# The start of a decoder kernel: first two row tiles multiplied before their norm is known

## Chip, core and metric

The kernel runs on one core of a Trainium2 chip. The metric is the device time of one execution in microseconds; the time before is 1604.12 us, the median of three runs.

## What is computed

One decoder layer on 1024 prompt rows and 8 sample rows of width 1024, all in 32-bit floats. Only the beginning of the mixer matters here: the rows are normed (rms norm with gain `mix_pre_g`), multiplied by `w_in`, and the second 1024 columns of the product, v, go through gelu and layer norm.

```python
def rms_norm(x, g):
    xf = x.astype(jnp.float32)
    y = xf * lax.rsqrt(jnp.mean(xf * xf, axis=-1, keepdims=True) + EPS)
    return (y * g.astype(jnp.float32)).astype(x.dtype)
...
    z = jnp.einsum("btd,dc->btc", xn, w_in)
    u, v, b_gate, c_gate, x_in, r_a, r_b = jnp.split(z, SPLITS, axis=-1)
    u = jax.nn.gelu(u)
    v = layer_norm(jax.nn.gelu(v), sgu_ln_g, sgu_ln_b)
    y_a = jnp.einsum("btc,cd->btd", u * chunk_spatial_mix(v, w_s, b_s), w_a_out)
```

The rest of the layer (the other parts of z, a short convolution, three output products, a gated feed-forward net) follows and is not changed.

## The kernel before

Every product of 32-bit numbers is made of three products of a faster format: each operand is split into a high part (a copy in the format f32r, made by ScalarE) and a low part (the number less its high part, made by VectorE or GpSimd), and high times high, low times high and high times low are added up in PSUM.

The program writes each engine's order out by hand; engines meet at counting semaphores. The stage at issue works through nine row tiles, `V_TILES`: position i = 0 is the tile of 8 sample rows, i = 1 to 8 are the prompt tiles of 128 rows. For each of them:

- SyncE's queue loads the rows (`x_load(i)`), into one of two buffers `x_rows`, and `wv_load(k)` loads the eight pieces of v's weight, 512 KB each, into `gv`.
- ScalarE sums the squares (`square(i)`) and splits off the high part of each weight piece (`wv_split(k)`).
- VectorE works out the reciprocal root in seven or eight one-column instructions (`row_root`), scales the rows by root and gain (`scale_rows(i)`, into `x_norm`), and makes the low parts of the weight (`wv_rest(k)`).
- TensorE turns the scaled rows, eight blocks (`turn_norm(i)`), ScalarE copies the high part from PSUM (`norm_split(i)`), VectorE makes the low part (`xn_rest(i)`, into `tp`).
- TensorE multiplies: `v_sample_tile` for the samples in the order of the table `V_STEPS`, `v_first_tile(1)` and `(2)` with all high products of a tile ahead of its low ones, then `v_tile(3)` to `(8)`, which wait for the low part before they start (`pe.wait_ge(xn_lo_done, i + 1)`). Each makes 48 products of 512 columns, and the turns of the next tile stand among them.
- ScalarE applies gelu and writes v, VectorE norms it (`v_layer_norm(i)`).

For VectorE the order from the second prompt tile on is this loop; the samples' own norm, with its gain and bias, is its pass i = 0:

```python
for i in range(9):
    if 0 < i < 8:
        xn_rest(i + 1)
    if 0 < i < 7:
        scale_rows(i + 2)
    if i < 8:
        v_layer_norm(i)
```

GpSimd has little to do here: it makes the identity matrix, copies the samples' split parts into `tp`, and masks `ws_rows`. Before its first real work TensorE turns the identity 32 times and 11 times (`turn_ident`).

Of the kernel before, what the change touches and what calls it, by code (L numbers as in the profile page):

```python
# [126 lines left out]
V_STEPS = [(0, 0), (0, 1), (1, 0), (0, 2), (1, 1), (0, 3), (1, 2), (0, 4), (1, 3), (0, 5), (0, 6), (1, 4), (0, 7), (1, 5), (1, 6), (1, 7)]  # L127
# [11 lines left out]
def build(nc, x_prompt, x_sample, state_conv, mix_pre_g, mix_post_g, w_in, sgu_ln_g, sgu_ln_b, w_s,  # L139
# [16 lines left out]
    with ctx:  # L156
# [62 lines left out]
        ws00 = at("ws00", sa_at + 1024, [128, KT])  # L219
        tail_out = s_bc[0:(2 + NS) * KT, 1].rearrange("p a c -> p (a c)")[:, 0:128]  # L220
# [12 lines left out]
        eps, warm = small[:, 46:47], small[:, 47:48]  # L233
        ps = ctx.enter_context(nc.psum_tensor("ps", [128, 8, 512], f32))
# [115 lines left out]
        wv_hi, wv_lo = sem("wv_hi"), sem("wv_lo")  # L350
# [58 lines left out]
        def _(pe):  # L409
# [7 lines left out]
            def turn_norm(i):  # L417
                rows = rows_of(V_TILES[i])
                pe.wait_ge(x_scaled, i + 1)
                if i >= 2:  # L420
                    pe.wait_ge(xn_lo_done, i - 1)
                for k in range(KT):
                    at_k = k ^ 1 if i and not home(V_TILES[i])[0] else k
                    ins = pe.transpose(ps[:, xn_bank(i) + k // 4, 128 * (at_k % 4):128 * (at_k % 4) + rows],  # L424
                                       x_norm[i % 2][0:rows, 128 * k:128 * k + 128], ident[0:rows, 0:rows])
                ins.then_inc(norm_turned, 1)

            def v_tile(i):
                t = V_TILES[i]
                pe.wait_ge(xn_lo_done, i + 1)  # L430
                if i >= 2:
                    pe.wait_ge(v_gelu, i - 1)
                for k in range(KT):
                    if k == 4 and i + 1 < 9:
                        turn_norm(i + 1)
                    outs = [ps[0:rows_of(t), 2 * (i % 2) + n, :] for n in range(2)]
                    w_h, w_l = ([w[:, k, 512 * n:512 * n + 512] for n in range(2)] for w in (wv_hi_t, wv_lo_t))
                    ins = three(outs, *xn_parts(t, k), w_h, w_l, k == 0, k == KT - 1)
                ins.then_inc(v_full, 1)

# [11 lines left out]
            def v_sample_tile():  # L452
                pe.wait_ge(xn_lo_done, 1)
                for low, k in V_STEPS:
                    x_h, x_l = xn_parts(8, k)
                    if low:
                        if k == KT - 2:
                            turn_norm(1)
                        pe.wait_ge(wv_lo, k + 1)
                        ins = wv_products(0, x_h, wv_lo_t, k, False, k == KT - 1)  # L460
                    else:
                        pe.wait_ge(wv_hi, k + 1)
                        wv_products(0, x_h, wv_hi_t, k, k == 0, False)
                        wv_products(0, x_l, wv_hi_t, k, False, False)
                ins.then_inc(v_full, 1)

            def v_first_tile(i):
                t = V_TILES[i]
                pe.wait_ge(xn_hi_done, i + 1)
                if i >= 2:  # L470
                    pe.wait_ge(v_gelu, i - 1)
# [302 lines left out]
        def _(sp):  # L774
            def x_load(i):
                t = V_TILES[i]
                if i >= 2:
                    sp.wait_ge(x_scaled, i - 1)
# [37 lines left out]
            x_load(0)  # L816
            sp.dma_start(pre_gain[0:NS, :], mix_pre_g[0:1, :].to_broadcast((NS, D))).then_inc(pre_first, 16)
            for k in range(KT):
                if k == 4:
                    x_load(1)  # L820
# [10 lines left out]
            sp.dma_start(ws_rows[:, :].rearrange("p (h j) -> p h j", h=KT), w_s[0].rearrange("h i j -> i h j")).then_inc(ws_in, 16)  # L831
            sp.dma_start(mix_b[:, :, :].rearrange("p h i -> p (h i)"),
# [6 lines left out]
            sp.dma_start(conv_sample[0, :, 0, :], state_conv[0, :, 1, :]).then_inc(hist_saved, 16)  # L839
            load(0)  # L840
# [227 lines left out]
        def _(pool):  # L1068
# [5 lines left out]
                               pattern=[[-1, 128]], channel_multiplier=1).then_inc(consts, 1)  # L1074
            for part, (smp, ready) in enumerate(((smp_hi, xn_hi_done), (smp_lo, xn_lo_done))):
# [124 lines left out]
        def _(act):  # L1200
# [15 lines left out]
            def norm_split(i):  # L1216
                act.wait_ge(norm_turned, i + 1)
# [45 lines left out]
            square(2)  # L1263
            for i in range(9):
                if 0 < i < 8:
                    norm_split(i + 1)
                if 0 < i < 7:
                    square(i + 2)
                act.wait_ge(v_full, i + 1)
                if i == 1:  # L1270
                    act.wait_ge(wv_lo, KT)
                rows = rows_of(V_TILES[i])
                dst = gv[:, V_TILES[i], :] if i else v_smp[0:NS, :]
                act.activation(dst.rearrange("p (a n) -> p a n", a=2), ps[0:rows, 2 * (i % 2):2 * (i % 2) + 2, :],
                               ACT.Gelu_apprx_tanh).then_inc(v_gelu, 1)
# [431 lines left out]
        def _(dve):  # L1707
# [16 lines left out]

            def row_root(i):
                rows = rows_of(V_TILES[i])
                a, y, w = (small[0:rows, 20 + n:21 + n] for n in range(3))
# [4 lines left out]
            def scale_rows(i, rooted=False):  # L1732
                rows, y = rows_of(V_TILES[i]), small[0:rows_of(V_TILES[i]), 21:22]
# [31 lines left out]

            scale_rows(0)
            wv_rest(0)
            xn_rest(0)
            for k in range(1, 4):
                wv_rest(k)  # L1770
            row_root(1)
            for k in range(4, 7):
                wv_rest(k)
            scale_rows(1, rooted=True)
            wv_rest(7)
            xn_rest(1)
            scale_rows(2)
            for i in range(9):
                if 0 < i < 8:
                    xn_rest(i + 1)  # L1780
                if 0 < i < 7:
                    scale_rows(i + 2)
                if i < 8:
                    v_layer_norm(i)
                if i == 0:
                    dve.wait_ge(v_norm, 1)
                    dve.wait_ge(ln_in, 32)
                    link(dve.tensor_tensor(v_smp[0:NS, :], v_smp[0:NS, :], ln_g[0:NS, :], MUL))
                    dve.tensor_tensor(v_smp[0:NS, :], v_smp[0:NS, :], ln_b[0:NS, :], ADD).then_inc(vs_ready, 1)
# [811 lines left out]
```

## Time and profile before

| what | value |
|---|---|
| time, median of 3 runs | 1604.12 us (1603.16 to 1604.5) |
| span of the profiled execution | 1601.0 us |
| TensorE busy | 1590.6 us, 99% |
| VectorE, ScalarE, GpSimd busy | 68%, 35%, 44% |

The profile gives the span of the profiled execution, from its first to its last instruction, and no separate time for it; the runs' median is 3.1 us above that span. In the rows further down PE is TensorE, DVE VectorE, ACT ScalarE, POOL GpSimd and SP SyncE. All starts are in us from the start of the span.

### The profile page before, as it was taken

How to read it: one execution, taken by the hardware profiler on the slowest of the kernel's cores; microseconds unless marked ns; L12 is line 12 of the kernel's file. 1: busy time of each engine (PE TensorE's matmuls, PEld its weight loads, DVE VectorE, ACT ScalarE, POOL GpSimd, SP SyncE). 2: the span in 40 equal slices, each digit the busy share in tenths (PEclk: the TensorE clock that was granted, in tenths of full speed). 3: DMA queues.
4: the chain of work that ended last, by engine and by line, in shares of the span. 5: the costliest groups of instructions: out<-in, count | busy, mean ns of one | idle time of the engine just before them, and what ended most of it. 6: DMA issues, size and time to landing. Idle time of an engine off the chain costs nothing.

```text
span 1601.0 us, 30253 instructions
## 1 busy us (share of the span) xinstructions
PE 1590.6 (99%) x12427; PEld 1542.2 (96%) x12427; DVE 1081.9 (68%) x1463; ACT 559.8 (35%) x852; POOL 703.9 (44%) x512
## 2 busy tenths in 40 slices
PE   9999999999999999999999999999999999999998
PEld 6889999999999999999978999999999999999997
DVE  8757857797793338868965666766666666575766
ACT  4222332222223336333434532333332233352544
POOL 1011534544544444644730324544444443545375
PEclk9999999999999999999999999999999999999999
DMA  6202011431423333474423313533333345472723
GB/s 216 79 1 80 27 54 34 126 96 44 126 82 110 109 106 121 149 242 133 148 91 120 131 41 110 155 105 100 106 104 104 105 124 178 153 239 80 238 107 133
DMA packets 155283, 184.38 MB, mean 115 GB/s; under 512 B 7355, under 2 KB 138035, under 8 KB 155147
## 3 DMA queue, kind: packets, MB, share of 16 engines
q1 hardware_dynamic: 154987, 182.41, 35.7%
q8 instruction: 99, 1.62, 0.4%
q14 instruction: 37, 0.30, 0.1%
q10 hardware_dynamic: 160, 0.04, 0.0%
HBM read 133.74 MB, written 48.72 MB: 114 GB/s over the span
## 4 chain that ended last, share of the span: by engine, by line
PE 95%; DVE 1%; DMA 1%; POOL 1%; issue 1%; SPq 0%; ACT 0%; DVEq 0%; ACTq 0%; POOLq 0%
PE ps L414 91%; PE ps L449 1%; PE ps L526 1%; DMA pre_gain<-in_mix_pre_g 1%; DVE tp L2213 1%; PE ps L669 0%; PE ps L653 0%; PE ps L424 0%; DMA tp_f<-hid_dram 0%; SPq L783 0%; DVE s_bc L2232 0%; POOL ring_lo L1108 0%; POOL ring_lo L1095 0%; PE ps L503 0%; DVE g L2234 0%
## 5 line engine op out<-in xcount | busy, mean ns | idle before, releaser
L414 PE MATMUL ps<-tp,ring_hi 128*128 128x258 f32 x7292 | 1182.9, 283 | 0.5 <-issue 0.3
L414 PEld LDWEIGHTS ps<-tp,ring_hi 128*128 128x128 f32 x7292 | 1010.6, 190 | 0.9 <-issue 0.5
L414 PE MATMUL ps<-tp,ring_lo 128*128 128x258 f32 x3646 | 744.8, 283 | 0.0
L414 PEld LDWEIGHTS ps<-tp,ring_lo 128*128 128x128 f32 x3646 | 571.3, 190 | 0.0
L1095 POOL TENSOR_TENSOR ring_lo<-ring_f,ring_hi 128x512 fp32r<-128x512 f32 (+1 forms) x228 | 328.3, 1460 | 365.1 <-DVE ring_f L1840 212.5
L1095 POOL TENSOR_TENSOR ring_lo<-stage,ring_hi 128x512 fp32r<-128x512 f32 (+1 forms) x199 | 304.7, 1540 | 400.3 <-ACT ring_hi L1240 399.6
L1240 ACT ACTIVATE ring_hi<-ring_f 128x512 fp32r<-128x512 f32 (+1 forms) x228 | 142.6, 627 | 519.9 <-DVE ring_f L1835 196.2
L1240 ACT ACTIVATE ring_hi<-stage 128x512 fp32r<-128x512 f32 (+1 forms) x199 | 122.0, 617 | 121.1 <-PE ps L414 63.5
L1832 DVE TENSOR_TENSOR ring_f<-stage 128x512 f32<-128x512 f32 (+1 forms) x57 | 46.8, 821 | 135.2 <-PE ps L414 82.7
L1853 DVE TENSOR_TENSOR s_a<-ps,s_a 128x516 f32<-128x516 f32 (+1 forms) x58 | 39.8, 686 | 51.9 <-PE ps L414 51.4
L414 PE MATMUL ps<-tp 128*128 128x512 f32 (+1 forms) x384 | 72.0, 340 | 0.0
L414 PEld LDWEIGHTS ps<-tp 128*128 128x128 f32 x384 | 59.0, 189 | 8.2
L2385 DVE TENSOR_TENSOR tp<-tp_f,tp 128x2064 fp32r<-128x2064 f32 (+1 forms) x24 | 56.2, 2343 | 13.7 <-ACT tp L1583 13.7
L1251 ACT ACTIVATE s_a<-ps 128x516 f32<-128x516 f32 (+1 forms) x58 | 34.2, 590 | 77.3 <-PE ps L414 60.2
L1864 DVE TENSOR_TENSOR s_a<-ps,s_a 128x516 f32<-128x516 f32 (+1 forms) x58 | 39.6, 683 | 30.5 <-PE ps L414 30.4
L1583 ACT ACTIVATE tp<-tp_f 128x2064 fp32r<-128x2064 f32 (+1 forms) x24 | 42.8, 1784 | 39.8 <-DMA tp_f<-hid_dram 33.2
L414 PE MATMUL ps<-wv_hi_t,tp 128*128 128x512 f32 x192 | 54.1, 397 | 0.0
L2420 DVE TENSOR_TENSOR hq<-hq,q 128x516 f32<-128x516 f32 x40 | 47.0, 1176 | 1.1
L1835 DVE TENSOR_TENSOR ring_f<-ring_f,stage 128x512 f32<-128x512 f32 (+1 forms) x57 | 42.8, 751 | 2.2 <-PE ps L414 2.2
L414 PEld LDWEIGHTS ps<-wv_hi_t,tp 128*128 128x128 f32 x192 | 35.7, 188 | 8.0
L1837 DVE TENSOR_TENSOR ring_f<-stage 128x512 f32<-128x512 f32 (+1 forms) x57 | 39.6, 695 | 0.0
L1847 DVE TENSOR_TENSOR s_bc<-ps,s_a 128x516 f32<-128x516 f32 (+1 forms) x21 | 14.0, 668 | 36.8 <-PE ps L414 36.6
(243 smaller groups left out, 1453.9 us busy)
## 6 DMA issues: line engine op xcount, KB each, us to landing
stage<-in_w_in SPq DMA_DIRECT2D x24, 1024.0 KB, 5.9
ht_dram<-ht SPq DMA_DIRECT2D x44, 258.0 KB, 4.2
hid_dram<-hq SPq DMA_DIRECT2D x40, 258.0 KB, 3.1
stage<-in_w_gate SPq DMA_DIRECT2D x10, 1024.0 KB, 6.6
stage<-in_w_up SPq DMA_DIRECT2D x10, 1024.0 KB, 5.3
tp_f<-hid_dram SPq DMA_DIRECT2D x16, 516.0 KB, 5.5
tp_f<-ht_dram SPq DMA_DIRECT2D x16, 516.0 KB, 8.7
stage<-in_w_down SPq DMA_DIRECT2D x8, 1024.0 KB, 7.1
```

The costliest lines, as they stand in the source:

```text
L414: ins = pe.matmul(o, w, xc, start=first and n == 0, stop=last and n == 2)
L1095: pool.tensor_tensor(lo, src, hi.bitcast(f32), SUB).then_inc(w_lo, 1)
L1240: act.activation(w_ring(b, p, kp)[0], src, ACT.Copy).then_inc(w_hi, 1)
L1251: act.activation(s_a[:, gs], reg(Z, gs), ACT.Copy).then_inc(s1_done, 1)
L1583: act.activation(slot(s, 0, both, ks), slot_f(s, 1, both, ks), ACT.Copy).then_inc(t_hi, 1)
L1832: ins = dve.tensor_tensor(out, a21, a22, ADD)
L1835: ins = dve.tensor_tensor(out, ring(ring_f, b, 1, kp), a11, SUB)
L1837: ins = dve.tensor_tensor(out, a11, a21, SUB)
L1853: dve.tensor_tensor(s_a[:, gs], reg(X, gs), s_a[:, gs], ADD).then_inc(u1_done, 1)
L1864: dve.tensor_tensor(s_a[:, gs], reg(Z, gs), s_a[:, gs], ADD).then_inc(u2_done, 1)
L2385: dve.tensor_tensor(slot(s, 1, both, ks), slot_f(s, 1, both, ks), slot_v(s, 0, both, ks), SUB).then_inc(t_lo, 1)
L2420: dve.tensor_tensor(hq[:, n], hq[:, n], q[:, n], MUL).then_inc(hid_ready, 1)
```

## The change

The samples and the first prompt tile are no longer scaled by their root before the product. The raw rows are turned at once (`turn_raw`), multiplied by the gain (turned into one column for each block, `gain_cols`), split, and multiplied; the root is applied as the scale of the gelu that reads the product. The normed, turned rows are still made as before, since later stages use them. Further:

- The samples' high parts (columns 0 to 7) and low parts (columns 32 to 39) stand in one tile, `smp_v`, of 40 columns, so that one product with the high weight gives both; the two groups of result rows are added afterwards, by a copy on ScalarE and a sum on VectorE.
- The steps of samples and first prompt tile are one table, `V_STEPS`: S is the 40-column product with a high weight piece, s the samples' with a low piece, H, L and l the prompt tile's three products, N a `turn_norm`; each of S, s, H, L, l is two products of 512 columns.
- GpSimd makes the low parts of weight pieces 3, 5 and 7; VectorE keeps 0, 1, 2, 4 and 6.
- The turns of the identity fall from 43 to 16.
- In VectorE's order the samples' layer norm stands behind `scale_rows(3)`.
- In SyncE's queue the first prompt tile is loaded right after the first weight piece; `x_load` of later tiles, `mix_b` and `load(0)` wait for the new steps.

```diff
-V_STEPS = [(0, 0), (0, 1), (1, 0), (0, 2), (1, 1), (0, 3), (1, 2), (0, 4), (1, 3), (0, 5), (0, 6), (1, 4), (0, 7), (1, 5), (1, 6), (1, 7)]
+V_STEPS = "S0 s0 S1 H0 H1 s1 S2 H2 L0 S3 H3 L1 S4 H4 s2 S5 H5 L2 s3 N0 H6 s4 S7 H7 s5 s6 L3 L4 L5 s7 S6 " \
+          "l0 l1 l2 N1 l3 l4 l5 L6 N2 L7 l6 l7".split()
+RAW_TURNS, RAW_SCALES = 2, 3
+WV_POOL = (3, 5, 7)
+WV_DVE = (0, 1, 2, 4, 6)
...
+            def v_start():
+                pe.wait_ge(consts, 5)
+                pe.wait_ge(x_scaled, 2)
+                for n, step in enumerate(V_STEPS):
+                    what, k = step[0], int(step[1])
+                    if what == "N":
+                        turn_norm(k)
+                    elif what == "S":
+                        pe.wait_ge(wv_hi, k + 1)
+                        ins = raw_products(32 + NS, 0, smp_v[:, k, :], wv_hi_t, k, n == 0, k == 6)
+                        if k == 6:
+                            ins.then_inc(v_full, 1)
+                    elif what == "s":
+                        wv_low_ready(k)
+                        raw_products(NS, 0, smp_v[:, k, 0:NS], wv_lo_t, k, False, False)
+                    elif what == "H":
+                        pe.wait_ge(raw_high, 1)
+                        pe.wait_ge(wv_hi, k + 1)
+                        raw_products(128, 2, raw_hi[:, k, :], wv_hi_t, k, k == 0, False)
+                    elif what == "L":
+                        pe.wait_ge(v_norm, 1)
+                        raw_products(128, 2, raw_lo[:, k, :], wv_hi_t, k, False, False)
                     else:
...
+                        wv_low_ready(k)
+                        ins = raw_products(128, 2, raw_hi[:, k, :], wv_lo_t, k, False, k == 7)
...
+            def turn_raw():
+                pe.wait_ge(x_in[0], 16)
+                pe.wait_ge(gain_in, 16)
+                for k in range(KT):
+                    pe.transpose(ps[:, 6, NS * k:NS * k + NS], x_rows[0][0:NS, 128 * k:128 * k + 128], ident[0:NS, 0:NS])
+                pe.transpose(ps[:, 6, NS * KT:NS * KT + KT], gain_rows[:, :], ident[0:KT, 0:KT]).then_inc(norm_turned, 1)
+                turn_ident(8)
+                pe.wait_ge(x_in[1], 16)
+                for k in range(KT):
+                    ins = pe.transpose(ps[:, 4 + k // 4, 128 * (k % 4):128 * (k % 4) + 128], x_rows[1][:, 128 * k:128 * k + 128], ident[:, :])
+                ins.then_inc(norm_turned, 1)
...
-            turn_ident(32)
-            turn_norm(0)
-            turn_ident(11)
-            v_sample_tile()
-            v_first_tile(1)
+            turn_ident(8)
+            turn_raw()
+            v_start()
             v_first_tile(2)
...
+            pool.memset(smp_v[:, :, NS:32].bitcast(f32), 0.0).then_inc(consts, 1)
+            for k in WV_POOL:
+                pool.wait_ge(wv_hi, k + 1)
+                pool.tensor_tensor(wv_lo_t[:, k, :], gv[:, k, :], wv_hi_t[:, k, :].bitcast(f32), SUB).then_inc(wv_lo_pool, 1)
...
             square(0)
             wv_split(0)
+            square(1)
             wv_split(1)
-            wv_split(2)
+            act.wait_ge(x_scaled, 3)
+            act.activation(raw_hi[:, :, :], raw_x[:, :, :], ACT.Copy).then_inc(raw_high, 1)
+            for k in range(2, KT):
+                wv_split(k)
             norm_split(0)
-            wv_split(3)
-            square(1)
-            for k in range(4, KT):
-                wv_split(k)
+            square(2)
+            act.wait_ge(v_full, 1)
+            act.activation(v_smp[0:NS, :].rearrange("p (a n) -> p a n", a=2), ps[32:32 + NS, 0:2, :], ACT.Copy).then_inc(v_gelu, 1)
             norm_split(1)
...
+            def v_norm_sample():
+                v_layer_norm(0)
+                dve.wait_ge(v_norm, 3)
+                dve.wait_ge(ln_in, 32)
+                link(dve.tensor_tensor(v_smp[0:NS, :], v_smp[0:NS, :], ln_g[0:NS, :], MUL))
+                dve.tensor_tensor(v_smp[0:NS, :], v_smp[0:NS, :], ln_b[0:NS, :], ADD).then_inc(vs_ready, 1)
...
+            wv_rest(0)
+            dve.wait_ge(norm_turned, 2)
+            dve.tensor_tensor(raw_x[:, :, :], bank_pair(4), gain_cols.unsqueeze(2).to_broadcast((128, KT, 128)), MUL).then_inc(x_scaled, 1)
+            wv_rest(1)
+            raw_rest()
+            wv_rest(2)
             scale_rows(0)
-            wv_rest(0)
+            wv_rest(4)
+            wv_rest(6)
+            row_root(1)
             xn_rest(0)
...
             scale_rows(1, rooted=True)
-            wv_rest(7)
+            scale_rows(2)
+            dve.wait_ge(v_gelu, 1)
+            dve.tensor_tensor(v_smp[0:NS, :].rearrange("p (a n) -> p a n", a=2), ps[0:NS, 0:2, :],
+                              v_smp[0:NS, :].rearrange("p (a n) -> p a n", a=2), ADD).then_inc(v_norm, 1)
             xn_rest(1)
-            scale_rows(2)
-            for i in range(9):
-                if 0 < i < 8:
+            for i in range(1, 9):
+                if i < 8:
                     xn_rest(i + 1)
-                if 0 < i < 7:
+                if i < 7:
                     scale_rows(i + 2)
+                if i == 1:
+                    v_norm_sample()
                 if i < 8:
                     v_layer_norm(i)
```

TensorE, the middle of the start sequence. Before, samples (`smp_hi`, `smp_lo`) are multiplied alone, and prompt products (`tp`) follow:

```order
L449 MATMUL ps<-wv_hi_t,smp_hi 8x512 x2
L449 MATMUL ps<-wv_hi_t,smp_lo 8x512 x2
L449 MATMUL ps<-wv_lo_t,smp_hi 8x512 x2
L424 MATMUL ps<-ident,x_norm_83 128x128 x8
L449 MATMUL ps<-wv_lo_t,smp_hi 8x512 x4
L449 MATMUL ps<-wv_hi_t,tp 128x512 x18
L449 MATMUL ps<-wv_lo_t,tp 128x512 x2
```

Now the steps from s3 to S6, with the turn of the samples' normed rows (`x_norm_82`) among them:

```order
L472 MATMUL ps<-wv_lo_t,smp_v 8x512 x2
L438 MATMUL ps<-ident,x_norm_82 128x8 x8
L472 MATMUL ps<-wv_hi_t,raw_hi 128x512 x2
L472 MATMUL ps<-wv_lo_t,smp_v 8x512 x2
L472 MATMUL ps<-wv_hi_t,smp_v 40x512 x2
L472 MATMUL ps<-wv_hi_t,raw_hi 128x512 x2
L472 MATMUL ps<-wv_lo_t,smp_v 8x512 x4
L472 MATMUL ps<-wv_hi_t,raw_lo 128x512 x6
L472 MATMUL ps<-wv_lo_t,smp_v 8x512 x2
L472 MATMUL ps<-wv_hi_t,smp_v 40x512 x2
```

Products of the prompt tile moved between those of the samples, and each product waits for its own weight part.

VectorE, around the samples' layer norm. Before, its last three passes (`v_smp`) stand directly ahead of the low part of the second prompt tile (`tp`):

```order
L1764 TENSOR_SCALAR v_smp<-v_smp,small 8x1024
L1788 TENSOR_TENSOR v_smp<-v_smp,ln_g 8x1024
L1789 TENSOR_TENSOR v_smp<-v_smp,ln_b 8x1024
L1752 TENSOR_TENSOR tp<-ps,tp 128x2x4x128
```

Now, with the one-column instructions of the roots left out at the dots, two low parts stand ahead of the scaling of the third prompt tile (`x_norm_83`), the samples' norm and that of the first tile (`gv`) behind it, and the next low part last:

```order
L1866 TENSOR_TENSOR v_smp<-ps,v_smp 8x1024
L1820 TENSOR_TENSOR tp<-ps,tp 128x2x4x128 x2
...
L1808 SCALAR_TENSOR_TENSOR x_norm_83<-x_rows_81,small,pre_gain 128x1024
L1826 BN_STATS small<-v_smp 8x6
...
L1832 TENSOR_SCALAR v_smp<-v_smp,small 8x1024
L1842 TENSOR_TENSOR v_smp<-v_smp,ln_g 8x1024
L1843 TENSOR_TENSOR v_smp<-v_smp,ln_b 8x1024
L1826 BN_STATS small<-gv 128x6
...
L1832 TENSOR_SCALAR gv<-gv,small 128x1024
L1820 TENSOR_TENSOR tp<-ps,tp 128x2x4x128
```

The samples' norm moved from ahead of the low part of the second prompt tile to ahead of that of the third.

## Rows read from the trace of the kernel before

**Rows 1.** The page: busy time (first three engines), and the chain by engine.

```profile
PE 1590.6 (99%) x12427; PEld 1542.2 (96%) x12427; DVE 1081.9 (68%) x1463; ACT 559.8 (35%) x852; POOL 703.9 (44%) x512
PE 95%; DVE 1%; DMA 1%; POOL 1%; issue 1%; SPq 0%; ACT 0%; DVEq 0%; ACTq 0%; POOLq 0%
```

**Rows 2.** TensorE's timeline (start, us, what), then a piece of the chain in time order.

```profile
1.76 5.87 PE L509 MATMUL ps<-ident 128*128 128x128 f32 x32 [1.76 <-POOL ident L1073]
...
9.35 0.69 PE L449 MATMUL ps<-wv_hi_t,smp_hi 128*8 128x512 f32 x2
...
22.05 4.46 PE L449 MATMUL ps<-wv_hi_t,tp 128*128 128x512 f32 x18 [0.19 <-ACT tp L1221]
...
34.16 4.34 PE L449 MATMUL ps<-wv_hi_t,tp 128*128 128x512 f32 x18
...
46.15 0.62 PE L414 MATMUL ps<-wv_hi_t,tp 128*128 128x512 f32 x2
...
52.71 11.17 PE ps L414 x48
```

**Rows 3.** Timeline of VectorE.

```profile
9.21 3.48 DVE L1744 TENSOR_TENSOR wv_lo_t<-gv,wv_hi_t 128x1024 fp32r<-128x1024 f32 x3
...
26.41 0.67 DVE L1758 BATCH_NORM_STATS2 small<-v_smp 8x6 f32<-8x512 f32 x1
...
30.73 1.21 DVE L1788 TENSOR_TENSOR v_smp<-v_smp,ln_g 8x1024 f32<-8x1024 f32 x1
31.98 2.09 DVE L1789 TENSOR_TENSOR v_smp<-v_smp,ln_b 8x1024 f32<-8x1024 f32 x1
34.00 1.21 DVE L1752 TENSOR_TENSOR tp<-ps,tp 128x1024 fp32r<-128x1024 f32 x1
...
38.37 0.69 DVE L1758 BATCH_NORM_STATS2 small<-gv 128x6 f32<-128x512 f32 x1
...
42.75 1.23 DVE L1752 TENSOR_TENSOR tp<-ps,tp 128x1024 fp32r<-128x1024 f32 x1
```

**Rows 4.** Timeline of ScalarE at the first weight pieces.

```profile
5.31 1.06 ACT L1214 ACTIVATE wv_hi_t<-gv 128x1024 fp32r<-128x1024 f32 x1 [1.39 <-DMA gv<-in_w_in]
6.58 1.06 ACT L1214 ACTIVATE wv_hi_t<-gv 128x1024 fp32r<-128x1024 f32 x1 [0.22 <-DMA gv<-in_w_in]
```

**Rows 5.** GpSimd's passes and VectorE's beside them, from five places.

```profile
9.10 3.65 POOL L1080 CAST tp<-smp_hi 128x16 fp32r<-128x16 f32 x4 [7.39 <-ACT smp_hi L1219]
31.91 1.09 POOL L1083 TENSOR_SCALAR_AFFINE_SELECT ws_rows<-ws_rows 128x1024 f32<-128x1024 f32 x1 [18.61 <-DMA ws_rows<-in_w_s]
110.43 3.00 POOL L1095 TENSOR_TENSOR ring_lo<-stage,ring_hi 128x512 fp32r<-128x512 f32 x2 [77.43 <-ACT ring_hi L1240]
110.64 0.27 DVE L1722 TENSOR_SCALAR small<-small 128x1 f32<-128x1 f32 x1
133.52 2.31 DVE L1806 TENSOR_TENSOR tp_f<-tp_f,tp 128x2064 f32<-128x2064 f32 x1
134.53 3.72 POOL L1095 TENSOR_TENSOR ring_lo<-stage,ring_hi 128x512 fp32r<-128x512 f32 x2 [18.61 <-ACT ring_hi L1240]
137.12 1.15 DVE L1891 TENSOR_TENSOR mix_s<-mix_s,q 128x4 f32<-128x4 f32 x1
138.87 0.15 DVE L1891 TENSOR_TENSOR mix_s<-mix_s,q 128x4 f32<-128x4 f32 x1
147.87 2.54 POOL L1095 TENSOR_TENSOR ring_lo<-stage,ring_hi 128x512 fp32r<-128x512 f32 x2 [9.61 <-ACT ring_hi L1240]
164.90 4.52 DVE L1821 TENSOR_TENSOR tp<-tp_f,tp 128x2064 fp32r<-128x2064 f32 x2
166.25 4.30 POOL L1095 TENSOR_TENSOR ring_lo<-stage,ring_hi 128x512 fp32r<-128x512 f32 x1 [7.76 <-ACT ring_hi L1240]
```

**Rows 6.** Stretches: us, TensorE busy (products and turns), other engines, PEclk, DMA, GB/s.

```profile
2.00:4.00 2.00, 2.00 (x11) 2.00 (x11) 0.06 (x1) 1.44 (x4) 0.00 (x0) 1.00 0.77 162
7.00:8.00 1.00, 1.00 (x13) 0.83 (x12) 1.00 (x2) 0.77 (x2) 0.00 (x0) 1.00 1.01 414
```

More of the change, by code:

```diff
@@ L450, in wv_products, with wv_low_ready @@
                 return ins
[L452 to L460, printed above, removed]
-                    else:
[L462 to L465, printed above, removed]
+            def wv_low_ready(k):
+                if k in WV_POOL:
+                    pe.wait_ge(wv_lo_pool, WV_POOL.index(k) + 1)
+                else:
+                    pe.wait_ge(wv_lo, WV_DVE.index(k) + 1)
@@ new lines, in raw_products @@
+            def raw_products(rows, bank, x, w, k, first, last):
+                for n in range(2):
+                    ins = pe.matmul(ps[0:rows, bank + n, :], x, w[:, k, 512 * n:512 * n + 512], start=first, stop=last)
+                return ins
+            def v_start():
[20 more added lines that the diff above has]
+                        raw_products(128, 2, raw_lo[:, k, :], wv_hi_t, k, False, False)
+                    else:
+                        wv_low_ready(k)
+                        ins = raw_products(128, 2, raw_hi[:, k, :], wv_lo_t, k, False, k == 7)
+                        if k == 7:
+                            ins.then_inc(v_full, 1)
@@ L816, in _ @@
             x_load(0)
+            sp.dma_start(gain_rows[:, :], mix_pre_g[0].rearrange("(k p) -> k p", p=128)).then_inc(gain_in, 16)
+            wv_load(0)
+            x_load(1)
+            wv_load(1)
             sp.dma_start(pre_gain[0:NS, :], mix_pre_g[0:1, :].to_broadcast((NS, D))).then_inc(pre_first, 16)
-            for k in range(KT):
-                if k == 4:
-                    x_load(1)
+            for k in range(2, KT):
                 wv_load(k)
@@ L839, in _ @@
             sp.dma_start(conv_sample[0, :, 0, :], state_conv[0, :, 1, :]).then_inc(hist_saved, 16)
+            sp.wait_ge(v_full, 2)
             load(0)
@@ L1268, in _ @@
                     square(i + 2)
+                rows = rows_of(V_TILES[i])
+                if i == 0:
+                    act.wait_ge(v_norm, 2)
+                    act.wait_ge(x_scaled, 1 + RAW_SCALES)
+                    act.activation(v_smp[0:NS, :], v_smp[0:NS, :], ACT.Gelu_apprx_tanh, scale=small[0:NS, 10:11]).then_inc(v_gelu, 1)
+                    continue
                 act.wait_ge(v_full, i + 1)
+                dst = gv[:, V_TILES[i], :].rearrange("p (a n) -> p a n", a=2)
+                src = ps[0:rows, 2 * (i % 2):2 * (i % 2) + 2, :]
                 if i == 1:
[L1271 to L1275, printed above, removed]
+                    act.wait_ge(wv_lo, len(WV_DVE))
+                    act.wait_ge(wv_lo_pool, len(WV_POOL))
+                    act.wait_ge(x_scaled, 2 + RAW_SCALES)
+                    act.activation(dst, src, ACT.Gelu_apprx_tanh, scale=small[:, 11:12]).then_inc(v_gelu, 1)
+                else:
+                    act.activation(dst, src, ACT.Gelu_apprx_tanh).then_inc(v_gelu, 1)
                 if i == 7:
@@ L1723, in newton, with root_of @@
                 link(dve.tensor_scalar(y, t, 1.5, y, ADD, MUL))
+            def root_of(i):
+                col = 10 + i if i < 2 else 21
+                return small[0:rows_of(V_TILES[i]), col:col + 1]
             def row_root(i):
                 rows = rows_of(V_TILES[i])
-                a, y, w = (small[0:rows, 20 + n:21 + n] for n in range(3))
+                a, y, w = small[0:rows, 20:21], root_of(i), small[0:rows, 22:23]
                 dve.wait_ge(sumsq, i + 1)
@@ L1732, in scale_rows @@
             def scale_rows(i, rooted=False):
-                rows, y = rows_of(V_TILES[i]), small[0:rows_of(V_TILES[i]), 21:22]
+                rows, y = rows_of(V_TILES[i]), root_of(i)
                 if not rooted:
```

60 lines of the change are left out of this document (34 added, 26 removed).

## The prediction

> **What bounds the kernel now.** The page's first lines and the chain that ended last come first: TensorE is busy 99% of the span and holds 95% of the chain [rows 1]. Whatever keeps TensorE's first products waiting is therefore paid in full at the end, and whatever the other engines save is worth nothing unless TensorE starts or continues earlier. Everything that the change touches lies ahead of 110 us. The timeline of TensorE there [rows 2] shows warm-up turns from 1.76 us, the sample products from 9.35, the first prompt tile's from 22.05, the second's from 34.16, the third's from 46.15 (12.0 us for a tile: later tiles show 11.17 for their 48 products, 0.465 for a pair, and the rest, 0.8 to 0.9, are the eight turns). There is one idle piece, 0.19 us. I call the point at 46.15 T: the products of `v_tile(3)` begin there, from there on nothing in the kernel changes, and TensorE has no idle time behind it in which a shift could be lost. So the forecast is the new T less 46.15.
>
> The timeline of VectorE [rows 3] tells what T hangs on. `v_tile(3)` waits for the fourth low part of turned rows (`xn_rest(3)`), which VectorE starts at 42.75 and ends near 43.95: 2.2 us of slack. VectorE was continuously busy from 34.00 to that point: low part, root and scale 4.37 (until 38.37), layer norm 4.38 (until 42.75). Its passes of 1024 columns take 1.16 each (3.48 for three).
>
> **What the change removes from TensorE.** A sample step was two high, two low-operand and two low-weight products; now the 40-column operand makes one pair do the first two. Sixteen of 96 products go, 8 pairs, 3.7 us. Samples and first tile are then 40 pairs, 18.5 us, plus three turns, some 2.4: 20.9 us. The start is nearer too: the second x piece is now requested before the second weight piece; in the old order the first two pieces of 512 KB landed at 5.31 and 6.58 [rows 4], so it should land near 6.6 and weight piece 1 at 7.9. Eight raw turns end at 7.5, VectorE's scaling of the raw tile at 8.7, and ScalarE, whose split of weight piece 1 ends at 8.95, makes the high part by 10.0. The first sample and prompt pairs run between; from 10.0 on 37 pairs and 2.4 us of turns are left, 19.5 us. If nothing else were late, the first tile would end at 29.6 instead of 34.16, a gain of 4.6 us.
>
> **What VectorE has to do.** It loses three weight low parts (3 x 1.16) to GpSimd and gets the scaled raw tile, its low part and the sum of the sample halves (1.16 each) and four small instructions (my estimate, 0.9 in all, from the 0.15 and 0.27 of the small passes in [rows 5]). It comes out even. But the order moves: the layer norm of the samples, 7.6 us in the old timeline (26.41 to 34.00, of which 0.9 is explained below), stood before `xn_rest(2)` and ended at 34.00, while TensorE was in the first prompt tile. Now it stands between `scale_rows(3)` and the first tile's layer norm, both ahead of `xn_rest(3)`. From the high part of tile 1 on, VectorE does 4.37 (low part, root, scale) + 6.8 (samples' norm: 4.32 to 30.73, then twice 1.24) + 4.38 + 1.18 = 16.7 us, and TensorE has only the second prompt tile, 12.0, before it needs the result. Since the high part comes 1.06 us after turn N2, and N2 is followed by three pairs (1.4 us), the end of the start sequence, E, gives T = E - 0.3 + 16.7 = E + 16.4, against E + 12.0 before. Of the 4.6 us gained, 4.4 are given back: T = 46.0, no change. This holds without any contention.
>
> **GpSimd's three low parts.** How GpSimd and VectorE meet is in [rows 5]. Alone, two passes of 512 columns took 2.54 us, 1.27 each. At 134.53 the same two took 3.72: the first began while VectorE's pass of two SBUF inputs (133.52 to 135.83) was running and got through only after it. At 137.12 VectorE's four-column pass, 0.15 us when repeated at 138.87, took 1.15 under GpSimd's second. At 31.98 the 8-row addition took 2.09 against 1.21 for the multiplication before it [rows 3], beside GpSimd's 1.09 pass at 31.91. The one-column passes of the roots are not held: at 110.64 one took its 0.27 under GpSimd's pass of 110.43. So passes with two SBUF inputs exclude each other. The Trainium skill says so too, in SBUF — State Buffer, section SBUF: two separate sides: the port pair shared by VectorE and GpSimd is an exclusive lock held for a whole instruction. By that rule the sum is the one below, without it the 46.0 above; the trace agrees with the rule.
>
> A low part of 1024 columns on GpSimd is not in the trace: twice 1.27 is 2.5, which I take; with overhead shared 2.3; from the pair at 110.43 (3.00, with VectorE beside it) 3.0. Who goes first when both wait? Casts of GpSimd got in between back-to-back VectorE passes of the same form as here (four in 3.65 us from 9.10, while VectorE ran three), but once a pass was held until the second of two VectorE passes ended (4.30 at 166.25, those from 164.90 to 169.42). I take turn and turn about. The walk: weight low part 2 on VectorE ends at 12.5; GpSimd's part 3 has it until 15.0; `scale_rows(0)`, ready at 14.4, until 16.2; part 5 until 18.7; VectorE's part 4 until 19.8; part 7 until 22.3; part 6 until 23.5. VectorE has waited 0.6 + 2.5 + 2.5 = 5.6 us. Then root and scale of rows 1 and 2 (with the samples' low part, 0.22) until 30.2, sum of samples 31.4, `xn_rest(1)` 32.5. TensorE waits 1.3 for part 4 (at 19.9) and 1.8 for part 6 (until 23.5), turns N2 at 30.4 and ends E near 32.2. ScalarE is held as well: its gelu of the samples waits for the sum (31.4 to 32.4), so the high part of tile 1 is ready at 33.4. T = 33.4 + 16.7 = 50.1, and TensorE has waited 0.7 and 4.7 more. That is +4.0.
>
> **The clock.** The granted clock reads 1.00 throughout, but the turns of `turn_ident` show two levels: 11 in 2 us at 2 to 4 us, 13 in 1 us at 7 to 8 [rows 6], by their ratio the levels 1.2 and 2.4 GHz; up to that rise TensorE had worked without a gap since 1.76. The new start has 16 such turns, not 43, and gaps. If the level is still low at 6.6, the raw turns cost 1.6 instead of 0.9 and everything behind them moves 0.6. I take half, 0.3. The Trainium skill (TensorE: Matmul & The Clock Gate, Part 1) has the throttled state as the default that activity releases, which would make these gaps count; the sum here goes by the rows.
>
> **Sum.** +4.0 + 0.3 = +4.3 us. The span was 1601.0, the median of the runs 1604.12, 3.1 above it; the same stands around both. Predicted 1608.4.
>
> **Rivals.**
> 1. VectorE keeps the port while it has work, as at 166.25: it does `scale_rows(0)` and parts 4 and 6 in a row until 18.5, GpSimd's part 5 ends at 21.0 and part 7 near 24.7. VectorE waits 0.6 + 0.3 + 0.5 only, TensorE 1.1 and 1.4; E is 32.1, T 48.5: +2.3, with the clock 2.6. 1606.7. For it the one row, against it the casts.
> 2. The port costs nothing here, T 46.0 (or GpSimd's parts come in VectorE's root chains): 1604 to 1605. Three places in [rows 5] speak against it.
> 3. The clock falls again in the wait of 4.7 us before T, or in those of 1.3 and 1.8. The trace has no such wait to price it; the first low stretch, from 1.76 to some point between 4 and 7, cost half of its length, 1.1 to 2.6 us, and I take as much for each fall: 1610 to 1613.
> 4. Faster: the 4.6 us are kept, 1599.5. That needs VectorE to reach `xn_rest(3)` before TensorE has done the second tile, so a tail of at most 12.3 us behind the high part of tile 1; the rows make it 16.7. It would come out so only if VectorE ran the sample norm inside its earlier idle time, which its program order excludes. Even with no wait at all VectorE's own passes from 7.5 add to some 36 us, T 43.9, 2.2 us of gain.
>
> **How the numbers follow.** Forecast (turn and turn about, 1607.8 for GpSimd passes of 2.3 to 1609.9 for 3.0, the clock's 0.3 included) 0.50; rival 1 0.20; rival 2 0.13; rival 3 0.12; rival 4 0.05. A measurement tells this kernel from no change at about 0.2%, 3.2 us. Slower by more: the forecast but for its low end (0.47), rival 3 (0.12), the upper end of rival 1 (0.04): 0.63. Faster by more 0.05. Same 0.32. The range leaves out rival 4 and part of rivals 2 and 3: 1604.8 to 1611.0.
>
> **What would show it.** The start sequence without the port would end at 29.6; I expect 32 to 33. VectorE's parts 4 and 6 (or GpSimd's 5 and 7) stretched to 3 us or more, TensorE idle 1 to 2 us before two low-weight pairs of the samples. Before `v_tile(3)` one wait of 4 to 5 us for VectorE's `tp`, T near 50. If that wait is absent, the step on the moved norm is wrong; if the parts are not stretched, that on the port. Turns of 0.2 us at 6.6 show the low clock.

## The result, and the profile after

The changed kernel takes 1610.12 us (median of five runs, 1609.24 to 1610.3) against 1604.12 before: ratio 1.0036, 95% interval 1.0024 to 1.0048. It is 6.0 us slower. Forecast were 4.3 us, with a range that ends at 1611.0.

The page after, the same two lines as in [rows 1]:

```profile
PE 1590.2 (99%) x12401; PEld 1541.8 (96%) x12401; DVE 1083.6 (67%) x1467; ACT 561.5 (35%) x854; POOL 711.1 (44%) x516
PE 93%; DVE 3%; POOL 1%; DMA 1%; issue 1%; ACT 1%; SPq 0%; DVEq 0%; ACTq 0%; POOLq 0%
```

TensorE's busy time hardly falls, though 16 products and 27 turns of the identity are gone (17 turns of raw rows and gain have come): some of its instructions ran slower. VectorE's share of the chain, 1% before, is 3%: the path leaves TensorE and goes through VectorE for some 17 us.

TensorE's timeline after, to be held against [rows 2]:

```profile
6.74 1.97 PE L512 MATMUL ps<-ident,x_rows 128*128 128x128 f32 x8
8.36 1.10 PE L472 MATMUL ps<-wv_hi_t,smp_v 128*40 128x512 f32 x2
...
11.12 1.19 PE L472 MATMUL ps<-wv_hi_t,raw_hi 128*128 128x512 f32 x4 [0.73 <-ACT raw_hi L1311]
...
24.77 0.64 PE L472 MATMUL ps<-wv_lo_t,smp_v 128*8 128x512 f32 x2 [0.90 <-POOL wv_lo_t L1127]
...
32.04 4.36 PE L461 MATMUL ps<-wv_hi_t,tp 128*128 128x512 f32 x18
...
48.61 1.22 PE L426 MATMUL ps<-wv_hi_t,tp 128*128 128x512 f32 x2 [4.41 <-DVE tp L1820]
49.63 1.05 PE L426 MATMUL ps<-wv_lo_t,tp 128*128 128x512 f32 x2
50.48 1.91 PE L426 MATMUL ps<-wv_hi_t,tp 128*128 128x512 f32 x4
```

The second prompt tile starts at 32.04, 2.1 us earlier than before; the third at 48.61, 2.5 us later, behind one wait of 4.41 us for VectorE. And the products behind the wait are slow: pairs start 0.85 to 1.02 us apart, not 0.46. In the chain (start, us, what) the 24 products ahead of the next turns took 8.11 us (7.95 in the timeline, from 48.61 to the turns at 56.56):

```profile
47.42 1.15 DVE tp L1820
48.57 0.04 issue
48.61 8.11 PE ps L426 x24
56.72 0.87 PE ps L438 x8
```

Before, the 24 products between 46.15 and the next turns took 5.5. So the second half of the third tile starts at 57.60 against 52.71 [rows 2]: 4.9 us are lost there, 2.46 because the tile starts later and 2.4 by slow products.

VectorE's timeline after, against [rows 3]:

```profile
15.32 1.50 DVE L1808 SCALAR_TENSOR_TENSOR x_norm<-x_rows,small,pre_gain 8x1024 f32<-8x1024 f32 x1
16.75 2.34 DVE L1812 TENSOR_TENSOR wv_lo_t<-gv,wv_hi_t 128x1024 fp32r<-128x1024 f32 x2
...
31.91 1.23 DVE L1820 TENSOR_TENSOR tp<-ps,tp 128x1024 fp32r<-128x1024 f32 x1 [1.48 <-ACT tp L1274]
...
36.30 0.67 DVE L1826 BATCH_NORM_STATS2 small<-v_smp 8x6 f32<-8x512 f32 x1
...
41.87 1.21 DVE L1843 TENSOR_TENSOR v_smp<-v_smp,ln_b 8x1024 f32<-8x1024 f32 x1
43.01 0.68 DVE L1826 BATCH_NORM_STATS2 small<-gv 128x6 f32<-128x512 f32 x1
...
47.34 1.22 DVE L1820 TENSOR_TENSOR tp<-ps,tp 128x1024 fp32r<-128x1024 f32 x1
```

From the low part of the second prompt tile at 31.91 to TensorE's start at 48.61 are 16.7 us without a gap in VectorE.

GpSimd's three low parts, each from its own stretch of the timeline:

```profile
13.05 2.69 POOL L1127 TENSOR_TENSOR wv_lo_t<-gv,wv_hi_t 128x1024 fp32r<-128x1024 f32 x1 [11.14 <-ACT wv_hi_t L1267]
15.71 5.64 POOL L1127 TENSOR_TENSOR wv_lo_t<-gv,wv_hi_t 128x1024 fp32r<-128x1024 f32 x1
21.32 3.39 POOL L1127 TENSOR_TENSOR wv_lo_t<-gv,wv_hi_t 128x1024 fp32r<-128x1024 f32 x1
```

The second was next at 15.71, when the first had ended, and itself ended at 21.35. VectorE's three passes of 15.32 to 19.09 (the scaling and two low parts, without a gap) went first; it ended 2.3 us after them. VectorE itself was hardly held: its two parts took 2.34 us, 1.17 each against 1.16 in [rows 3].

Last the stretches of TensorE's slow products (columns as in [rows 6]), after:

```profile
44.00:48.60 4.60, 0.20 (x1) 0.00 (x0) 4.25 (x13) 1.02 (x1) 0.00 (x0) 0.80 0.20 71
48.60:52.00 3.40, 3.39 (x8) 2.71 (x9) 3.12 (x10) 0.00 (x0) 0.00 (x0) 0.50 0.00 0
52.00:56.00 4.00, 4.00 (x15) 3.16 (x15) 3.65 (x12) 0.00 (x0) 0.00 (x0) 0.80 0.41 135
```

The granted clock stands at 0.50, 1.2 GHz, from 48.6 to 52. It fell in the wait: the mean of the stretch that holds the wait is already 0.80.

### The profile page after: what moved, and what is told of

The parts are those of the page before. It is cut to its first block, busy times and chain, and to the rows that moved or that the text cites. A ratio compares the mean times of both kernels' runs of the same rounds, so it can differ in the third digit from the quotient of the medians.

```text
span 1608.4 us, 30225 instructions
## 1 busy us (share of the span) xinstructions
PE 1590.2 (99%) x12401; PEld 1541.8 (96%) x12401; DVE 1083.6 (67%) x1467; ACT 561.5 (35%) x854; POOL 711.1 (44%) x516
## 4 chain that ended last, share of the span: by engine, by line
PE 93%; DVE 3%; POOL 1%; DMA 1%; issue 1%; ACT 1%; SPq 0%; DVEq 0%; ACTq 0%; POOLq 0%
PE ps L426 90%; PE ps L571 1%; POOL wv_lo_t L1127 1%; DVE tp L2301 1%; DMA stage<-in_w_in 1%; PE ps L714 0%; PE ps L698 0%; PE ps L438 0%; DMA tp_f<-hid_dram 0%; DMA x_rows<-in_x_prompt 0%; POOL ring_lo L1148 0%; PE ps L472 0%; DVE s_bc L2320 0%; POOL ring_lo L1161 0%; DVE small L1786 0%
```

## The experiments

Single runs lie up to 1 or 2 us to either side of their median, so medians and intervals of 5 to 11 runs are compared, each with runs of the kernel before on the same chip. Differences to the changed kernel are differences of medians from two chips; where one is under 1 us, the traces are the better witness.

**The samples' norm moved again (e1).** It is cut in two and goes behind the first tile's:

```diff
-                if i == 1:
-                    v_norm_sample()
+                if i == 2:
+                    v_layer_norm(0)
+                if i == 3:
+                    v_gain_sample()
                 if i < 8:
                     v_layer_norm(i)
```

> The changed kernel with the samples' layer norm moved once more and cut in two: its norm stands in VectorE's pass 2, its gain and bias in pass 3. Theory A (VectorE's own chain from the high part of prompt tile 1 on, 16.7 us, is what TensorE waits for): the wait of 4.4 us before the third prompt tile's products is gone, they begin at E + 12.0 = 44.0 us, the clock does not fall, and both costs (4.4 and 2.5 us) come back: about 1603 us, some 7 us less than the changed kernel and 1 us less than the one before. Rival B (the start is late because GpSimd and VectorE hold each other's port, and the norm's place only hides that): the wait stays at 2 us or more, 1606 us or more. If the slack that remains in passes 2 and 3 is too small, a wait of about 1 us moves to the fourth or fifth tile.

Measured: 1602.44 us against 1603.91, ratio 0.999 (0.9981 to 0.9999), 7.7 us less than the changed kernel. TensorE's timeline at the third tile:

```profile
43.83 0.63 PE L461 MATMUL ps<-wv_lo_t,tp 128*128 128x512 f32 x2
44.30 0.62 PE L426 MATMUL ps<-wv_hi_t,tp 128*128 128x512 f32 x2
44.77 0.63 PE L426 MATMUL ps<-wv_lo_t,tp 128*128 128x512 f32 x2
```

No wait, no slow products, and none at the fourth or fifth tile either. The whole loss was the place of this norm; the start itself, with its wait of 0.88 us for GpSimd's last part, is 1.85 us earlier at the third tile than before (44.30 against 46.15).

**All weight low parts on VectorE (e2),** in the changed kernel:

```diff
-WV_POOL = (3, 5, 7)
-WV_DVE = (0, 1, 2, 4, 6)
+WV_POOL = ()
+WV_DVE = (0, 1, 2, 3, 4, 5, 6, 7)
...
             wv_rest(2)
+            wv_rest(3)
             scale_rows(0)
-            wv_rest(4)
-            wv_rest(6)
+            for k in range(4, KT):
+                wv_rest(k)
             row_root(1)
```

> The changed kernel with all eight weight low parts on VectorE, in the order of the pieces; GpSimd makes none. Theory A: the wait of 0.9 us for GpSimd's last part goes, VectorE has 3.5 us more to do and ends its second scaling near 29, still ahead of turn N2, so the tail is the same: 1609 to 1610.5 us, within 1 us of the changed kernel. Rival B (the port held the start back): the start sequence ends 2 us earlier or more and the time falls by as much, 1608 us or less.

Measured: 1609.41 us, ratio to before 1.0035 (1.0022 to 1.0047). TensorE:

```profile
48.74 0.79 PE L426 MATMUL ps<-wv_hi_t,tp 128*128 128x512 f32 x2 [4.40 <-DVE tp L1820]
49.33 1.05 PE L426 MATMUL ps<-wv_lo_t,tp 128*128 128x512 f32 x2
```

The same wait, at the same place. Taking GpSimd's three parts away does not make T earlier. The clock fell here too, but only behind the wait: the first pair is still fast, the second slow, and the two stretches read 1.00 and then 0.60 (columns as in [rows 6]):

```profile
44.00:48.60 4.60, 0.34 (x2) 0.00 (x0) 4.25 (x12) 1.02 (x1) 0.00 (x0) 1.00 0.15 49
48.60:52.00 3.40, 3.26 (x9) 2.58 (x10) 3.12 (x11) 0.00 (x0) 0.00 (x0) 0.60 0.02 5
```

**TensorE kept busy in the wait (e3).**

```diff
+            turn_ident(36)
             for i in range(3, 9):
                 v_tile(i)
```

> The changed kernel with 36 turns of the identity ahead of the third prompt tile's products, inside the wait of 4.4 us: TensorE's work and the point at which those products can begin (48.6 us) are the same, but it is not idle. Theory C (2.5 of the 6 us are the clock that fell in the wait): the 24 products behind the wait take 5.6 us instead of 8.1 and the time falls by 2.5, to 1607.6 us. Rival (the slow products have another cause, such as reading data just written): they stay at 8.1 us and the time at 1610 us.

Measured: 1605.95 us, ratio 1.0013 (1.0004 to 1.0022), 4.2 less than the changed kernel by the medians. TensorE's timeline:

```profile
44.11 4.09 PE L556 MATMUL ps<-ident 128*128 128x128 f32 x36
48.67 0.73 PE L426 MATMUL ps<-wv_hi_t,tp 128*128 128x512 f32 x2 [0.47 <-DVE tp L1821]
49.24 0.62 PE L426 MATMUL ps<-wv_lo_t,tp 128*128 128x512 f32 x2
```

The stretch in which the clock was 0.50 (columns as in [rows 6]):

```profile
48.60:52.00 3.40, 3.33 (x14) 2.74 (x15) 3.12 (x11) 0.00 (x0) 0.00 (x0) 1.00 0.00 0
```

The products begin at 48.67, no earlier than the 48.61 of the changed kernel, at a granted clock of 1.00; the 24 take 5.8 us in the chain. The next tile half starts at 55.32 in its chain instead of 57.60: 2.3 us, the size expected. The medians say more than the trace; the chip of this comparison gave some 0.2 us of it (its runs of before are 0.2 faster), the rest stays open.

**Only the norm moved, in the kernel before (e4).** Its first loop pass has no `v_layer_norm(0)`; norm, gain and bias stand in pass 1 behind `scale_rows(3)`:

```diff
-                if i < 8:
-                    v_layer_norm(i)
-                if i == 0:
+                if i == 1:
+                    v_layer_norm(0)
                     dve.wait_ge(v_norm, 1)
...
+                if 0 < i < 8:
+                    v_layer_norm(i)
```

> The kernel before with only the samples' norm, gain and bias moved behind the scaling of the third prompt tile. Theory A: VectorE's chain from the high part of prompt tile 1 (30.7 us) is 16.7 us long, so the third tile's products begin at 47.5 instead of 46.15 us, a wait of 1.3 us; the clock holds: 1605.4 us. Rival B: no wait, 1604.1 us.

Measured: 1605.91 us, ratio 1.0014 (1.0005 to 1.0023), 2.0 us more than before. TensorE:

```profile
47.33 0.73 PE L414 MATMUL ps<-wv_hi_t,tp 128*128 128x512 f32 x2 [1.17 <-DVE tp L1752]
```

Expected were 1.3 us of wait at 47.5. Where TensorE comes later to this place, the same tail costs only what sticks out; the granted clock stays at 1.00 through this wait of 1.17 us. The third tile starts 1.2 us later than before; the rest of the 2.0 is not traced to a place, and the interval (0.8 to 3.7 us) includes 1.2.

**All low parts on VectorE, with the norm cut in two (e5).** The norm as in e1, and the edit of e2:

```diff
-WV_POOL = (3, 5, 7)
-WV_DVE = (0, 1, 2, 4, 6)
+WV_POOL = ()
+WV_DVE = (0, 1, 2, 3, 4, 5, 6, 7)
```

> The kernel with the samples' norm cut in two, and all eight weight low parts on VectorE. TensorE is now the bound of the tail, so its own waits count: the wait of 0.9 us for GpSimd's last part goes, a wait of 0.15 at turn N2 and one of 0.7 ahead of the second prompt tile (seen in the trace with the late norm) come. Theory A: the same as with GpSimd's parts, within 0.5 us, some 1602.2 us; handing three parts to GpSimd buys nothing. Rival: VectorE, loaded with 3.5 us more, makes TensorE wait 2 us or more: 1604 us.

Measured: 1602.32 us against 1603.65, ratio 0.9992 (0.9983 to 1.0001); e1 had 0.999. TensorE has the two waits that were expected, and none for a part:

```profile
29.09 1.09 PE L438 MATMUL ps<-ident,x_norm 128*128 128x128 f32 x8 [0.23 <-DVE x_norm L1808]
32.29 4.42 PE L461 MATMUL ps<-wv_hi_t,tp 128*128 128x512 f32 x18 [0.71 <-ACT tp L1274]
```

Handing three parts to GpSimd buys nothing: its late part costs 0.9 us, VectorE's load without it 0.9, and the third tile starts at 44.36 against 44.30 in e1.

**s7 later (e6),** on top of e1:

```diff
-V_STEPS = "S0 s0 S1 H0 H1 s1 S2 H2 L0 S3 H3 L1 S4 H4 s2 S5 H5 L2 s3 N0 H6 s4 S7 H7 s5 s6 L3 L4 L5 s7 S6 " \
-          "l0 l1 l2 N1 l3 l4 l5 L6 N2 L7 l6 l7".split()
+V_STEPS = "S0 s0 S1 H0 H1 s1 S2 H2 L0 S3 H3 L1 S4 H4 s2 S5 H5 L2 s3 N0 H6 s4 S7 H7 s5 s6 L3 L4 L5 l0 l1 s7 S6 " \
+          "l2 N1 l3 l4 l5 L6 N2 L7 l6 l7".split()
```

> The kernel with the samples' norm cut in two, and in the table of steps l0 and l1 ahead of s7 and S6. Theory A: the 0.9 us in which TensorE waited for GpSimd's last part are filled by the two pairs, and the time falls by 0.9, to 1601.5 us. Rival: the samples' result comes no later, but ScalarE and VectorE behind it (copy, sum, gelu, high part of tile 1) are now the bound and the second prompt tile waits for them: 1602.4 us, no gain.

Measured: 1601.51 us against 1603.65, ratio 0.9984 (0.9976 to 0.9993). TensorE at the place of the old wait:

```profile
23.66 1.07 PE L472 MATMUL ps<-wv_lo_t,raw_hi 128*128 128x512 f32 x4
24.73 0.62 PE L472 MATMUL ps<-wv_lo_t,smp_v 128*8 128x512 f32 x2
25.19 0.62 PE L472 MATMUL ps<-wv_hi_t,smp_v 128*40 128x512 f32 x2
```

The 0.9 us are gone, and the third tile starts at 43.04, 1.3 us ahead of e1. The medians agree, but the intervals of e1 and e6 overlap. Of the kernels run this has the lowest ratio to the one before, 2.1 us by the medians, with e7 within its noise. At the third tile it is 3.1 us ahead of the kernel before, so about 1 us does not reach the end: its trace has later waits of 0.8 and 0.5 us where before has 0.3 and 0.3.

**More full turns first (e7),** on top of e1: 16 turns ahead of the samples' and 2 behind, instead of 8 and 8.

```diff
-                turn_ident(8)
+                turn_ident(2)
                 pe.wait_ge(x_in[1], 16)
...
             pe.wait_ge(consts, 4)
-            turn_ident(8)
+            turn_ident(16)
             turn_raw()
```

> The kernel with the samples' norm cut in two, and the 16 turns of the identity all but two ahead of the samples' turns, so that TensorE turns full blocks without a gap until 5.2 us. Theory C (the low clock at the start is the price of less work in its first microseconds; before the change the turns were fast from 6.3 us on, after it only from 9.3): the raw turns at 6.7 us take 0.9 instead of 1.6 us, the first pair 0.5 instead of 0.9, and the raw tile's chain starts 0.4 to 0.8 us earlier, the time falls by up to that, to 1602 us; the wait for GpSimd's last part may take it back. Rival: the clock rises at 9.3 us again: 1602.4 us.

Measured: 1601.5 us, ratio 0.9986 (0.9977 to 0.9995). But the trace does not show what the theory says. TensorE:

```profile
6.90 1.91 PE L512 MATMUL ps<-ident,x_rows 128*128 128x128 f32 x8
8.47 1.20 PE L472 MATMUL ps<-wv_hi_t,smp_v 128*40 128x512 f32 x2
9.47 0.82 PE L472 MATMUL ps<-wv_lo_t,smp_v 128*8 128x512 f32 x2
```

The raw turns take 1.9 us as before this edit, the first pair is slow, and the third tile starts within 0.2 us of e1's (44.17). The time is below both forecasts, but the interval overlaps that of e1. The theory on where the early clock comes from is not supported.

**GpSimd's three parts alone, in the kernel before (e8).**

```diff
+            for k in WV_POOL:
+                pool.wait_ge(wv_hi, k + 1)
+                pool.tensor_tensor(wv_lo_t[:, k, :], gv[:, k, :], wv_hi_t[:, k, :].bitcast(f32), SUB).then_inc(wv_lo_pool, 1)
...
-            for k in range(4, 7):
+            for k in (4, 6):
                 wv_rest(k)
             scale_rows(1, rooted=True)
-            wv_rest(7)
```

> The kernel before with only GpSimd's three low parts (of pieces 3, 5 and 7). Theory A: GpSimd passes of 2.3 us, held by VectorE's passes, give part 7 near 20 to 21 us, where TensorE wants it at 21.2; nothing on TensorE's path moves: 1604 us, within 1. Rival B (the port makes VectorE late): the scaling of rows 1, wanted at 19.7, or part 7 comes 1 us or more late: 1605 us or more.

Measured: 1606.49 us against 1603.65, ratio 1.0017 (1.0008 to 1.0026). The rival was right. VectorE's timeline:

```profile
15.83 5.20 DVE L1753 TENSOR_TENSOR wv_lo_t<-gv,wv_hi_t 128x1024 fp32r<-128x1024 f32 x2
20.95 1.27 DVE L1749 SCALAR_TENSOR_TENSOR x_norm<-x_rows,small,pre_gain 128x1024 f32<-128x1024 f32 x1
```

And TensorE's:

```profile
22.28 1.09 PE L426 MATMUL ps<-ident,x_norm 128*128 128x128 f32 x8 [2.51 <-DVE x_norm L1749]
```

GpSimd's passes beside them:

```profile
14.19 2.42 POOL L1082 TENSOR_TENSOR wv_lo_t<-gv,wv_hi_t 128x1024 fp32r<-128x1024 f32 x1 [1.41 <-ACT wv_hi_t L1222]
17.24 2.70 POOL L1082 TENSOR_TENSOR wv_lo_t<-gv,wv_hi_t 128x1024 fp32r<-128x1024 f32 x1 [0.64 <-ACT wv_hi_t L1222]
```

Two VectorE passes take 5.20 us instead of 2.34. The first waits for the end of GpSimd's pass of 14.19; the second, which starts at 17.6, takes 3.4 us, because GpSimd's pass of 17.24 gets in between the two and ends at 19.94. So here the engines did take turns, as the forecast had assumed for the new start. TensorE waits 2.5 us for the scaled rows, and the third tile starts at 48.59, 2.4 us later than before. The same three GpSimd passes cost 2.8 us here and none on balance in the new start.

**The 40-column product undone (e9, e10).** High and low parts of the samples in two products of 8 columns; the two halves of the sum are then half the result each, so that ScalarE and VectorE do the same passes:

```diff
-                        ins = raw_products(32 + NS, 0, smp_v[:, k, :], wv_hi_t, k, n == 0, k == 6)
+                        raw_products(NS, 0, smp_v[:, k, 0:NS], wv_hi_t, k, n == 0, False)
+                        ins = raw_products(NS, 0, smp_v[:, k, 32:32 + NS], wv_hi_t, k, False, k == 6)
```

On top of e6 (e9):

> The kernel with the samples' norm cut in two and s7 late, and the 40-column product undone: high and low parts of the samples are multiplied by the high weight in two products of 8 columns each (16 products more, 3.7 us of TensorE). Theory: TensorE is the bound of this start, so nearly all of it is paid, 3.7 less the 0.4 us that it waited anyway: 1604.8 us against 1601.5. Rival (TensorE still has hidden waits in its start that the extra products fill): 1603 us or less.

In the changed kernel (e10):

> The changed kernel with the 40-column product undone in the same way. The tail that makes TensorE wait 4.4 us starts at turn N2, which stands in TensorE's own order, behind the added products; VectorE was ready 4 us before it. Theory: the added 3.7 us move N2 by 2.8 (0.9 fill the wait for GpSimd's last part) and the tail with it: 1612.9 us. Rival (the tail starts on VectorE's side, so TensorE's saving was worth nothing here): 1610 us.

Measured: e9 1604.35 us, ratio 1.0004 (0.9995 to 1.0013), 2.8 us more than e6. e10 1611.23 us, ratio 1.0046 (1.0033 to 1.0059), 1.1 more than the changed kernel; its third tile:

```profile
50.23 1.22 PE L426 MATMUL ps<-wv_hi_t,tp 128*128 128x512 f32 x2 [4.40 <-DVE tp L1821]
```

The tail moved by 1.6 us, not 2.8 and not 0, and the wait stayed 4.40. The added products first filled the two waits of the changed kernel's start (0.73 and 0.90 in its timeline; counted from the start of one pair to the next, 0.9 and 1.1), more than I had counted. The tail starts on TensorE's side, as the theory has it, and its size was off. The third tile of e9:

```profile
46.16 0.62 PE L426 MATMUL ps<-wv_hi_t,tp 128*128 128x512 f32 x2
```

That is 3.1 us behind e6 (43.04) and where the kernel before has it (46.15). So what the new start gains with the norm in a good place and s7 late is gone without the 40-column product. Whether that product alone, in the old order, would give the same gain was not run.

## Why the prediction was right, and where not

**The moved norm: right, to 0.1 us.** The 16.7 us that the prediction gave VectorE from the high part of tile 1 on measured 16.70 (31.91 to 48.61). That T hangs on this chain is shown by e1 (the wait goes), e2 (it stays without GpSimd's passes) and e4 (a wait appears when nothing but the norm is moved).

**The start: right in sum, wrong in its parts.** E was to be near 32.2; the second tile began at 32.04. The x piece landed in time, but the raw turns took 1.6 us, at the low clock, and the first prompt product came at 11.12 instead of 10.0; the sum had 0.3 for this. The waits of 1.3 us for part 4 and 1.8 for part 6 did not come; there was one of 0.90 for part 7. Of the 2.4 us between the 29.6 of the undisturbed sum and 32.04, then, 1.1 are the late first product, 0.9 to 1.1 that wait, and the rest small gaps. That the sum of the waits came out near is luck. (The working also puts the wait ahead of the second tile at 0.7 where its own times, 32.2 and 33.4, make 1.2; T does not depend on it, and the trace has no such wait.)

**The port: the exclusion right, the order wrong.** The step that failed is "I take turn and turn about". VectorE kept the port through its three passes, as rival 1 had it, which was to give T 48.5; it was 48.61. Rival 1 was near in part by chance too: it had TensorE wait 1.1 and 1.4 us for parts, where the trace has 0.90 and a later first product. VectorE was not held for 5.6 us, the high part of tile 1 not late, and the forecast's T of 50.1 is 1.5 too high. The rows of before could not settle the order: casts got in between VectorE's passes, the row with two inputs at 166.25 [rows 5] did not, and in e8 GpSimd's passes with two inputs did get in between. What decides it is open. Nor do both sides need two inputs, as the prediction has it: the GpSimd pass at 31.91 [rows 5] that it counts as holding VectorE reads one. A GpSimd pass of 1024 columns took 2.3 us once VectorE had let go (19.09 to 21.35), and 2.42 in e8, near the lower bound that I named.

**The clock: the cost right, its chance too low.** Rival 3 priced a fall in the long wait at 1.1 to 2.6 us and gave it 0.12. It fell and cost 2.4; e3 shows that it was the wait: filled with turns, the clock stayed at 1.00 with T unchanged. It fell also in e2 and e10, each with a wait of 4.4 us and 24 products of 7.4 and 7.2 us in the chain, against 5.8 in e3; in e2 the fall came only behind the wait, after one fast pair. The Trainium skill (TensorE: Matmul & The Clock Gate, Part 1) says that the throttled state is the default and activity releases it; by that rule the long wait was to be priced as a cost, not as a rival. The three traces with a wait of 4.4 us agree with it.

So the forecast of +4.3 stood on a third tile 4.0 us late, all of it put down to the port, and left out the fall of the clock. The tile was 2.5 us late, with GpSimd's three passes (48.61) and with them on VectorE (48.74, e2): the start gained 2.1 us, and the moved norm made the stretch from E to T 4.6 longer. The clock added 2.4. The two errors nearly cancelled; that the measured 6.0 lies inside the range is in part luck. What T would be with GpSimd's passes and no contention, which the prediction put at 46.0, no run shows. At 110 us the two traces are 4.9 apart. The profiled executions as a whole are 7.4 us apart (spans of 1608.4 and 1601.0), the medians 6.0. The remaining 1.1 us to the 6.0 of the medians is only argued: the after trace has two waits of 0.62 and 0.75 us, at 486 and 819, of which before shows 0.3, and such late waits differ from trace to trace of the experiments too. No run tells whether the shift causes them.

**Rival 4** (4.6 us kept, 1599.5) needed VectorE's tail within 12.3 us. e1 takes the sample norm out of it and gets 44.3 for T, not 41.5: with the low clock and the wait for part 7 the start sequence had kept 2.1 of the 4.6.

## What to carry to other kernels

When a start is rearranged, follow the engine that comes second on the path past the rearranged piece until its slack before the next tile is known. Here the step that cost all the gain, a norm of 8 rows, was moved by one tile, and 6.8 us of VectorE work counted in full while TensorE's tile had 2.2 us of room. A wait that long on TensorE should be priced with the low clock behind it. And before work is given to GpSimd, look which VectorE passes with two SBUF inputs run beside it, and on which of them TensorE waits: the same three passes cost nothing in one order and 2.8 us in another.

## What was not expected of the hardware

- Who goes first is not fixed. In the changed kernel a GpSimd pass that was next at 15.71, with VectorE's scaling already waiting since 15.32, waited for that and for two more VectorE passes behind it (5.64 us for a pass of 2.3). In e8 a GpSimd pass that came at 17.24, in the middle of the first of two VectorE passes, got in ahead of the second (two passes in 5.20 instead of 2.34 us).
- The granted clock does not show the low level of the first microseconds: it reads 1.00 from 0 to 9 us in every trace, while the same turns take 0.20 us each before some point and 0.11 behind it. That point was near 6 us in the trace of before and at about 4.5 in that of e4, whose TensorE program starts with the same 32 turns (they took 5.87 and 5.02 us). In the traces with the new start it lay anywhere from 8.4 (e2, whose first pair is fast) to past 10.3 (e3, whose third pair, at 10.26, still takes 0.86 us); 16 full turns in a row at the beginning (e7) did not bring it forward. What sets it is open, and it differs between traces of the same start.
- Behind the wait of 4.4 us the clock was at 0.50 from 48.6 to 52 us. In a wait of the same length in e2 it had not fallen yet when the work went on, and it fell 0.6 us later. After one of 1.2 us (e4) it had not fallen, and 24 products took 5.8 us.
